# Chunks of qkv and units of the output projection woven between the heads of the two last attentions

## The reference, cut to what matters

```python
# layer i of the second block
q, k, v = rotary((h @ w_qkv) ...)            # 16 or 12 heads of 64; rotary on q and k
s   = q @ k.T * 64 ** -0.5                   # + causal mask, or the mask of the head's group
p   = exp(s - lse);  o = p @ v               # for i=0 o / sum(p)
alpha = softmax over the 3 groups of lse     # i=1 alone; per row and head slot
mix = (o * alpha) @ w_o
h = layer_norm(ALPHA * h + mix)
h = layer_norm(ALPHA * h + square(relu(h @ w_in)) @ w_out)
```

## Time and profile before

| | us |
|---|---|
| median of three runs | 1570.93 (1565.92 to 1571.12) |
| the profiled execution | 1568.38 |
| its span | 1566.6 |
| TensorE busy | 1488.0 (95%) |
| GpSimd busy | 1218.8 (78%) |
| ScalarE busy | 711.0 (45%) |
| VectorE busy | 693.9 (44%) |

### The profile page before, as it was taken

One profiled execution on the slowest core, in us unless ns is written; L12 is line 12 of the kernel. 1 busy time (PEld: TensorE's weight loads), 2 busy tenths in 40 slices (PEclk: granted clock), 3 DMA queues, 4 the chain that ended last, 5 costly groups with the idle time before them and its releaser, 6 DMA issues.

```text
span 1566.6 us, 20124 instructions
## 1 busy us (share of the span) xinstructions
PE 1488.0 (95%) x7206; PEld 1217.8 (78%) x7206; DVE 693.9 (44%) x1364; ACT 711.0 (45%) x1068; POOL 1218.8 (78%) x984
## 2 busy tenths in 40 slices
PE   4998998999999999999899999999999999899997
PEld 3786887688887887877688887877888878778886
DVE  7656754554633558634433103354331043543212
ACT  3334553454344435543544444464554345455442
POOL 4789985798797976555898897925999978189994
PEclk9998999999999999998999999999999999899999
DMA  9896544699885985434587565733665656156553
GB/s 360 307 356 182 171 133 124 206 326 295 281 284 167 357 285 174 135 97 132 174 253 230 162 213 163 214 106 107 189 187 188 201 175 212 39 153 196 180 189 107
DMA packets 168239, 313.85 MB, mean 200 GB/s; under 512 B 13366, under 2 KB 19914, under 8 KB 168138
## 3 DMA queue, kind: packets, MB, share of 16 engines
q1 hardware_dynamic: 166384, 311.21, 61.9%
q10 hardware_dynamic: 1754, 1.35, 0.4%
HBM read 311.45 MB, written 1.06 MB: 199 GB/s over the span
## 4 chain that ended last, share of the span: by engine, by line
PE 81%; DVE 8%; POOL 4%; DMA 3%; ACT 2%; issue 1%; SPq 0%; DVEq 0%; ACTq 0%
PE bank L671 70%; POOL lo_units L632 4%; DMA ada_units<-in_ada_w 2%; PE bank L811 2%; PE bank L1957 2%; PE bank L829 1%; DMA raw_units<-in_w_in 1%; DVE bank L1351 1%; PE bank L845 1%; PE bank L726 1%; PE bank L798 1%; PE bank L800 1%; PE bank L799 1%; ACT hi_units L1042 1%; DVE turned L1406 1%
## 5 line engine op out<-in xcount | busy, mean ns | idle before, releaser
L632 POOL TENSOR_TENSOR lo_units<-raw_units,hi_units 128x512 fp32r<-128x512 f32 (+2 forms) x944 | 1168.9, 1274 | 312.9 <-ACT hi_units L1042 311.9
L671 PE MATMUL bank<-hi_units,turned 128*128 128x512 f32 (+2 forms) x2784 | 873.9, 390 | 13.2 <-DVE turned L1446 4.4
L1042 ACT ACTIVATE hi_units<-raw_units 128x1024 fp32r<-128x1024 f32 (+2 forms) x478 | 484.8, 1018 | 545.5 <-PE bank L671 471.0
L671 PEld LDWEIGHTS bank<-hi_units,turned 128*128 128x128 f32 x2784 | 522.1, 190 | 122.6 <-issue 5.7
L671 PE MATMUL bank<-lo_units,turned 128*128 128x512 f32 (+2 forms) x1392 | 535.5, 385 | 0.0
L671 PE MATMUL bank<-hi_units,turned_wide 128*128 128x512 f32 x992 | 315.3, 393 | 4.4 <-POOL lo_units L632 4.4
L671 PEld LDWEIGHTS bank<-lo_units,turned 128*128 128x128 f32 x1392 | 265.4, 191 | 49.7 <-issue 2.4
L671 PEld LDWEIGHTS bank<-hi_units,turned_wide 128*128 128x128 f32 x992 | 186.2, 188 | 48.6 <-POOL lo_units L632 8.5
L671 PE MATMUL bank<-lo_units,turned_wide 128*128 128x512 f32 x496 | 193.2, 389 | 0.0
L1351 DVE SCALAR_TENSOR_TENSOR bank<-ada_units,small,bank 128x512 f32<-128x512 f32 x132 | 99.7, 756 | 54.8 <-DMA ada_units<-in_ada_w 50.8
L671 PEld LDWEIGHTS bank<-lo_units,turned_wide 128*128 128x128 f32 x496 | 93.2, 188 | 18.9 <-issue 0.7
(11 more groups left out here) (210 smaller groups left out, 1162.6 us busy)
## 6 DMA issues: line engine op xcount, KB each, us to landing
raw_units<-in_w_in SPq DMA_DIRECT2D x104, 512.0 KB, 5.1
ada_units<-in_ada_w SPq DMA_DIRECT2D x88, 512.0 KB, 7.3
raw_units<-in_w_ffn_in SPq DMA_DIRECT2D x80, 512.0 KB, 4.4
raw_units<-in_mlp_w_in SPq DMA_DIRECT2D x64, 512.0 KB, 3.7
raw_units<-in_mlp_w_out SPq DMA_DIRECT2D x64, 512.0 KB, 3.3
raw_units<-in_w_ffn_out SPq DMA_DIRECT2D x44, 512.0 KB, 4.2
raw_units<-in_moba_w_qkv SPq DMA_DIRECT2D x24, 512.0 KB, 4.3
raw_units<-in_w_out SPq DMA_DIRECT2D x16, 512.0 KB, 4.4
```

The source lines that it names most:

```text
L632: pool.tensor_tensor(LO[:, s, b, 0:w], RAW[:, u["slot"], b, 0:w], HI_[:, s, b, 0:w].bitcast(F32), ALU.subtract).then_inc(lo_ready.sem, lo_ ...
L671: ins = pe.matmul(BANK[2 * c["pair"] + t][:, 0:w], xs[:, part, :], W[:, s, b, 0:w], start=(i == 0 and m == 0 and q == 0), stop=(i == len(c ...
L1042: act.activation(HI_[:, s, 0:n, 0:w], RAW[:, u["slot"], 0:n, 0:w], ACT.Copy)\
```

## The change

The qkv chunks of the second block get a new cut and order: an A chunk holds q and k of four heads (two transfers of 256 KB for each unit), a V chunk 512 columns of v. Only the first three (i=0) or two (i=1) run ahead of the attention. The rest is woven between its steps by the table WOVEN, and for i=0 units and half units of wo as well. O is turned in groups of four heads (O_TURNS), some of them inside the attention, to a tile of its own, OT. DVE drains the woven chunks, and makes the low part of turned O, in `late(k)`, after `put_out` and `copy_turned` of the step. The delays become score=1, turn=3, weigh=4; scores lie in two banks, turned probabilities in one for i=0, in up to four for i=1; ACT's copies of them go to DVE. For i=1 the minimum over the groups is found in step 12, the weights in step 13, ten heads of O are multiplied then and the last two as they are put out. Of residual(wo 0) tile 1 moves into `norm(0)`. The second half of wo begins its first tile while the first half is not done.

```diff
+QKV_ORDER = (("A0", "V0", "A1", "A2", "V1", "A3"), ("A0", "V0", "A1", "A2", "V1"))
+QKV_AHEAD = (3, 2)
+WOVEN = (
+    {0: (("A2", 0, BOTH),), 1: (("A2", 1, BOTH),), 2: (("A2", 2, BOTH),), 3: (("A2", 3, BOTH),),
+     4: (("V1", 0, BOTH),), 5: (("V1", 1, BOTH),), 6: (("V1", 2, BOTH),), 7: (("V1", 3, BOTH),),
+     8: (("A3", 0, BOTH),), 9: (("A3", 1, BOTH),), 10: (("A3", 2, BOTH), ("A3", 3, BOTH)),
+     11: ((0, 0, (0,)),), 12: ((0, 0, (1,)),), 13: ((1, 0, (0,)),), 14: ((0, 1, (0,)),), 15: ((0, 1, (1,)),),
+     16: ((1, 1, (0,)),), 18: ((0, 2, (0,)),), 19: ((0, 2, (1,)),)},
+    {0: (("A1", 0, BOTH), ("A1", 1, BOTH)), 1: (("A1", 2, BOTH), ("A1", 3, BOTH)),
+     2: (("A2", 0, BOTH),), 3: (("A2", 1, BOTH),), 4: (("A2", 2, BOTH),), 5: (("A2", 3, BOTH),),
+     6: (("V1", 0, BOTH),), 7: (("V1", 1, BOTH),), 8: (("V1", 2, BOTH),), 9: (("V1", 3, BOTH),)})
+O_TURNS = ({9: 0, 13: 1, 17: 2}, {14: 0, 15: 1})
...
-    TWO = dict(score=3, turn=5, weigh=7, qk=QKT2, pt=PT2, n_pt=3, n_qk=3, sb=(SB_, (0, 2)), tp=(TP, 3, 1), act_copies=True)
+    TWO = [dict(score=1, turn=3, weigh=4, qk=QKT2, pt=PT2, n_pt=3, n_qk=3, tp=tp)
+           for tp in ((TP,) * MOBA_H, (TP,) * 5 + (*aside, TP, *aside, TP, SB_[0]))]
...
             def turn_head(h):
                 if real(h):
                     pe.wait_ge(exped.sem, exped.at((tag, h)))
-                    if real(h - n_tp):
-                        pe.wait_ge(head_out.sem, head_out.at((tag, h - n_tp)))
+                    if real(tp_user_before(pipe, h)):
+                        pe.wait_ge(head_out.sem, head_out.at((tag, tp_user_before(pipe, h))))
...
+                    if one["kind"] in "MD":
+                        if k % 4 == 0:
+                            pe.wait_ge(drained.sem, drained.at(("qkv", tag[1], f"A{k // 4}")))
+                        if k - 1 in O_TURNS[tag[1]]:
+                            pe.wait_ge(turned_lo.sem, turned_lo.at((("o2", tag[1]), O_TURNS[tag[1]][k - 1])))
...
+            def weave(k, i=i):                       # TensorE
+                if k in O_TURNS[i]:
+                    turn_o(O_TURNS[i][k])
+                for what, u, tiles in WOVEN[i].get(k, ()):
+                    if isinstance(what, str):
+                        unit(by_key["qkv", i, what], u, HT, tiles)
+                    else:
+                        out_unit(by_key["wo", i, what], u, tiles)
...
+            if i == 0:
+                turn_o(3)
+                out_unit(wo1, 2, (0,))
+                out_unit(wo0, 3)
+                out_unit(wo1, 3, (0,))
+            else:
+                out_unit(wo0, 0)
+                turn_o(2)
+                out_unit(wo0, 1)
+                out_unit(wo1, 0, (0,))
+                out_unit(wo1, 1, (0,))
+                out_unit(wo0, 2)
+                out_unit(wo1, 2, (0,))
...
+            def weave(k, i=i):                       # ACT
+                prep(first + given[0] + 4)
+                given[0] += sum(tiles[-1] == NT - 1 for what, _, tiles in WOVEN[i].get(k, ()))
...
+            attention(("two", i), heads, weave, TWO[i])
+            prep(first + given[0] + 5)
+            turn_hi_o(len(heads) // 4 - 1)
...
                 else:                                # DVE, end of a step
                     put_out(k - pipe["weigh"])
                     copy_turned(k - pipe["turn"])
+                    late(k)
...
+            def late(k, i=i):
+                for what, u, tiles in WOVEN[i].get(k, ()):
+                    if isinstance(what, str) and u == KT // UNIT_K - 1:
+                        qkv_out(what)
+                if i == 1 and k == nh:
+                    group_max()
+                if i == 1 and k == nh + 1:
+                    group_weights()
+                if k in O_TURNS[i]:
+                    turn_lo_o(O_TURNS[i][k])
...
             def norm(t):
                 say(v.bn_aggr(MV[:, 2 * t:2 * t + 2], STAT[:, 12 * t:12 * t + 12]), ("var", (tag, t)))
+                if t == 0 and rest:
+                    residual(rest, (1,))
```

More of the change, by code:

```diff
@@ L274, in plan @@
         heads = (MOBA_H, DIL_H)[i]
-        w = 3 * heads * DH
-        for j in range(-(-w // CW)):
-            n = min(CW, w - j * CW)
-            put(chunk(("qkv", i, j), (("moba_w_qkv", "dil_w_qkv")[i],), 0, KT, j * CW, n))
+        for name in QKV_ORDER[i]:
+            n = int(name[1:])
+            if name[0] == "A":
+                cols, width = (4 * n * DH, heads * DH), CW
+            else:
+                cols, width = 2 * heads * DH + n * CW, min(CW, heads * DH - n * CW)
+            put(chunk(("qkv", i, name), (("moba_w_qkv", "dil_w_qkv")[i],), 0, KT, cols, width))
         for cc in range(2):
@@ L498, in raw_ready @@
     def raw_ready(e, u):
-        e.wait_ge(raw_in[u["slot"]], 16 * (u["turn"] + 1))
+        e.wait_ge(raw_in[u["slot"]], u["landed"])
     def ada_raw(u):
@@ L986, in _ @@
             beginning(("x", i), X, x_rows(i), HT)
-            gemms(HT, until=("qkv",))
-            pe.wait_ge(drained.sem, drained.at(("qkv", i, -(-3 * len(heads) * DH // CW) - 1)))
-            attention(("two", i), heads, QKV, lambda k: None, TWO)
-            turn_and_start(("o2", i), O, lambda g: (rows, "weighted") if i else (head_out, (("two", 0), len(heads) - 1 if g else 3)),
-                           HT, len(heads) * DH // P)
+            for _ in QKV_ORDER[i][1:QKV_AHEAD[i]]:
+                c = todo.pop(0)
+                for u in range(len(c["units"])):
+                    unit(c, u, HT)
@@ new lines, in _, with turn_o @@
+            n_groups = len(heads) // 4
+            wo0, wo1 = by_key["wo", i, 0], by_key["wo", i, 1]
+            def turn_o(g, i=i):
+                if i == 0:
+                    pe.wait_ge(head_out.sem, head_out.at((("two", 0), 4 * g + 3)))
+                elif g < 2:
+                    pe.wait_ge(rows.sem, rows.at("weighted"))
+                else:
+                    pe.wait_ge(head_out.sem, head_out.at((("two", 1), 4 * g + 3)))
+                for t in range(NT):
+                    for j in range(2):
+                        ins = pe.transpose(o_bank(i, g)[:, (j * NT + t) * P:(j * NT + t + 1) * P],
+                                           O[:, t, (2 * g + j) * P:(2 * g + j + 1) * P], con("ident"))
+                ins.then_inc(turned.sem, turned.mark((("o2", i), g)))
@@ new lines, in _ @@
+            attention(("two", i), heads, QKV, weave, TWO[i])
+            while todo[0]["key"][0] in ("qkv", "wo"):
+                todo.pop(0)
+            if i == 0:
+                turn_o(3)
+                out_unit(wo1, 2, (0,))
+                out_unit(wo0, 3)
+                out_unit(wo1, 3, (0,))
+            else:
+                out_unit(wo0, 0)
[5 more added lines that the diff above has]
+                out_unit(wo1, 2, (0,))
@@ L1119, in attention @@
         def attention(tag, heads, weave, pipe):
-            for k in range(len(heads) + (pipe["turn"] if pipe["act_copies"] else pipe["score"])):
+            for k in range(len(heads) + (pipe["weigh"] if heads[0]["kind"] in "MD" else pipe["score"])):
                 weave(k)
@@ L1263, in _, with turn_hi_o @@
             heads = heads_two(i)
-            for j in range(-(-3 * len(heads) * DH // CW)):
-                prep_chunk(("qkv", i, j))
-            attention(("two", i), heads, lambda k: None, TWO)
-            if i == 1:
-                act.wait_ge(rows.sem, rows.at("group_max"))
-                act.activation(MX[:, 0:3 * 4 * NT], NM[:, 0:3 * 4 * NT], ACT.Exp, scale=-1.0)\
-                    .then_inc(act_side.sem, act_side.mark("group_exp"))
-            turn_hi(("o2", i), HT, len(heads) * DH // P)
+            for name in QKV_ORDER[i][:QKV_AHEAD[i]]:
+                prep_chunk(("qkv", i, name))
+            first = by_key["qkv", i, QKV_ORDER[i][QKV_AHEAD[i]]]["units"][0]["index"]
+            given = [0]
+            def turn_hi_o(g, i=i):
+                act.wait_ge(turned.sem, turned.at((("o2", i), g)))
+                act.activation(OT[:, 2 * g:2 * g + 2, 0, :], o_bank(i, g)[:, :].rearrange("p (k s) -> p k s", k=2), ACT.Copy)\
+                    .then_inc(turned_hi.sem, turned_hi.mark((("o2", i), g)))
+            def weave(k, i=i):
+                prep(first + given[0] + 4)
+                given[0] += sum(tiles[-1] == NT - 1 for what, _, tiles in WOVEN[i].get(k, ()))
+                if i == 1 and k == len(heads) + 1:
+                    act.wait_ge(rows.sem, rows.at("group_max"))
+                    act.activation(MX[:, 0:3 * 4 * NT], MX[:, 0:3 * 4 * NT], ACT.Exp, scale=-1.0)\
+                        .then_inc(act_side.sem, act_side.mark("group_exp"))
+                if k in O_TURNS[i]:
+                    turn_hi_o(O_TURNS[i][k])
+            attention(("two", i), heads, weave, TWO[i])
+            prep(first + given[0] + 5)
+            turn_hi_o(len(heads) // 4 - 1)
             prep_chunk(("wo", i, 0))
@@ L1892, in _ @@
[L1892 to L1911 removed]
```

(3 more changed lines are left out.)

165 lines of the change are left out of this document (92 added, 73 removed).

## The result

The changed kernel takes 1593.82 us (median of four runs, 1592.52 to 1596.94), the kernel before on the same chip 1570.66: ratio 1.0153, 95% interval 1.0140 to 1.0167, or 23.2 us slower. The profiled execution took 1596.94 us, its span is 1595.1, against 1566.6 of before: 28.5 us. I had forecast 14.2 us more, with a range that ended at 1592.

The account below looks back on a forecast made before the run. TensorE, 95% busy, was taken as the bound, with 21 us idle or slow within reach. Terms 8.4 + 1.0 - 1.0 + 4.0 + 1.8 = +14.2 us on 1568.4 gave 1582.6, stated as 1583; range 1557 to 1592.

Parts of the forecast that it names:

- LayerNorm: LayerNorm behind wo: tile 1's moved residual delays the chain, 0.9 us for each i, bounds 0 and 1.4.
- The waits of i=0: Attention of i=0: TensorE waits behind DVE's drains, copies and turned O, 13.4 us in sum.
- unit 17: Second unit of wo half 1, i=0: prepared only in step 16 behind exp(14), about 1.0 us late.
- The waits of i=1: Attention of i=1: TensorE waits 2.0 and 3.3 behind drains, 0.5 for copies, 5.9 in the last steps.
- the tail: Six last steps of i=1's attention, no unit left after k=9: 5.9 us of waits.
- The clock: TensorE at half clock after waits: 1.0 us lost in i=0 (0 or 2), 4.0 in i=1 (0 to 5.5).
- the 4.8 us wait: Kernel before, i=1: TensorE waits for the weighted rows; forecast to shrink to 2.2 us.
- Rival 3: Clock falls in i=0 too, staying down over half-unit steps: 10 us more, 1593; chance 0.10 shared with rival 4.
- The work itself: TensorE's pieces in both stages: 77.8 us plus 2.0 for restarts at i=0, 61.5 plus 1.5 at i=1.
- The DMA: Second transfer of each A unit: costed at 0, about 7 us if the cover of five slots were gone.
- Rival 4: Second DMA makes A units late: +7 us at most, 1590; chance 0.10 shared with rival 3.
- The rival that the cover works: Weaving hides DVE's drains in both attentions: i=0 wins 5 us, i=1 wins 8, 1555 us; chance 0.15.

## Why the prediction was wrong

It had the sign and the mechanism, and named each wait. It was 9 us short by the medians (14.2 forecast, 23.2 measured), and 1.8 us outside its range. The 1583 that I gave was the sum for the profiled run; on the median of before the same sum makes 1585. I take its steps in the profiled execution, where the miss is 1596.9 less 1582.6, 14.3 us. By the stages of the prediction, i=0 ran from the end of the prefix at 996.2 to 1095.3, 99.1 us for a forecast of 93.2 + 1.0; i=1 from 1311.5 to 1396.3, 84.8 for 74.7 + 4.0. So 4.9 of the miss are in i=0, 6.1 in i=1, 3.6 in unchanged code, nothing in LayerNorm, and 0.3 the other way elsewhere.

**The waits of i=0: right.** Forecast 13.4. Measured 12.8: turns 4.8 for 5.3, transposes 3.0 for 2.8, copies 3.9 for 3.7, turned O 0.7 for 0.6, unit 17 0.4 for 1.0. Walking DVE's queue step by step, with durations of before, gave sizes within a few tenths of a us.

**The waits of i=1: right, a little high.** Forecast 11.7 (2.0 + 3.3 + 0.5 + 5.9), measured 10.3: the scores 2.3 for 2.8 (2.0, and the 0.8 behind V1's drain in the tail), the turn 3.0 for 3.3, the copies 3.7 for 3.4 (0.5, and 2.9 of the tail's 5.9), and the product with the weights 1.3 for 2.2.

**The clock: the term that failed.** I took 1.0 for i=0 and 4.0 for i=1, with an upper end of 2 and 5.5. The chain shows 3.1 and 9.4, so 7.5 us of the miss lie here. I had asked whether the clock falls in the tail and perhaps once more. It fell after three of the four waits behind a drain, and in the tail for the whole of 1371 to 1386. The size was also low: for one fall behind a wait I took 1.5 to 2, and they were 1.8, 2.9 and 3.1; for the tail I took 4 at most, and it was 4.7. The row for the right size was there, 5.20 for 2.72, 2.5 us for the first unit alone; I read it as a property of the 4.8 us wait. The slow stretch of before at 1325, behind waits of 1.0 and 0.7, would have told me otherwise. The kernel with the waits filled shows the term from the other side: 10 us back by the ratios and 11.8 by the stages, with all of DVE's queue as it was, where the chain says 12.5. Rival 3 (the clock falls in i=0 too, 1593) gave the right time. Its mechanism did happen in i=0, but once and for 3 us, not over the 28 us of half-unit steps; most of the clock's cost was in i=1. That its time fits is luck. In the kernel without the drains' rotary the clock did fall in those steps, for 11 us, so the rival was a real one.

**The work itself: a little low.** What is left, 3.4 us in i=0 and 2.1 in i=1 (4.9 less 2.1 of clock plus 0.6 of waits; 6.1 less 5.4 plus 1.4), is in the pieces. The short pieces are not it: scores 0.63 and 0.22, transposes 0.44, two turns of 0.34 and two products of 0.80 and 0.87 make 3.64 for a pair, and I had counted 3.38 and 0.25 for the restarts. The units are: the eleven full units of i=0 that stand on the chain take 31.1 us, 2.82 each for my 2.72, which is 1.2 us over twelve, and the half units at full clock take 1.38 to 1.50 for my 1.36. The rest I have not followed further.

**LayerNorm: right in the sum.** 0.9 each was forecast. From the first residual of the second half to the last low part it is 15.7 us for 15.0 at i=0, and 15.2 for 14.1 at i=1. But putting the residual back did not recover it, so my reason for it, the moved residual, is not shown. What else differs is that the first half ends 1.5 us ahead of the second's first tile, where before it was 5.4; that this is the cause is argued, not shown.

**The DMA: right.** The transfers of 256 KB cost nothing: no wait of TensorE ends on a transfer, and units' waits for GpSimd are 0.4 us in all. Rival 4 falls.

**The rival that the cover works: not as built.** With A3 before V1, split drains and the product after the unit, the cover does work at i=0 (126.9), and it comes out even with before, not the 5 us ahead that this rival gave; at i=1 it is 5.3 behind the kernel that has the early weights alone. The Trainium skill, "Perfetto Trace Analysis", section "Optimization Strategy", says that interleaving regimes may improve a kernel. Against the same pipeline with nothing woven in it does, by 31.7 us, much of which goes with the clock; against a pipeline that was already deep, no run here shows a gain from it.

## What to carry to other kernels

When a chunk of matrix work is woven into a pipeline, walk the queue of the engine that drains it. Every drain is one piece, and it delays the copy behind it by its whole length (4.3 us here); split it and put it after what TensorE is waiting for, and look at the order within a step before looking at the totals. Price a wait of TensorE with the clock that may fall behind it: here three waits of 1.9 to 3.0 us cost 1.8 to 3.1 more, about as much again, a tail of waits of at most 1.3 us cost 4.7, and a fourth wait of 1.9 us cost nothing more. If you fill a wait with matmuls that nobody reads, keep them shorter than the wait: twelve of them in a wait of 1.5 us pushed the work behind by 1.2. And measure the parts of a compound change alone: of this one the early group weights gained 0.35% by themselves, while the bundle lost 1.5%.

## What I had not expected of the hardware

The length of a wait does not tell whether the clock falls. After the 1.9 us wait in step 4 of i=0 it stayed up, and after one of 1.9 in step 3 of i=1 it fell, as the next units show. The chain of the changed kernel at the first of these (the unit at 1330.01, above, is the second, with 4.53):

```profile
1016.84 0.52 PE bank L842 x3
...
1019.02 2.81 PE bank L702 x12
```

The step before the second was two units (5.5 us of dense work); before the first there was dense work too. I can't say from these rows what tells them apart. The same holds for the last half-unit steps of i=0: with the same waits and the same work the clock stayed at 1.00 in the change and was 0.54 in the kernel without the drains' rotary. Matmuls whose result nobody reads kept it at 1.00 over both stages in all three kernels whose profile shows them. In the kernel with 48 of them TensorE still waited 0.2 to 0.7 us behind the larger groups, so these delayed nothing; in the other two the last group was longer than its wait and pushed the turn of O by 0.9 and 1.2 us.
